# Hybrid attention step on one core: where a head's small products stand between the tile products

## The chip, the core and the metric

The kernel runs on one core of a Trainium2 chip. The core has a matrix engine (PE, whose weight loads the profile lists apart as PEld), a vector engine (DVE), a scalar engine (ACT), GpSimd (POOL) and SyncE (SP); each runs its own list of instructions in order, and they wait for each other through semaphores. The metric is the device time of one launch in microseconds (us), median of several runs. The profile is one execution taken with the hardware profiler.

## The reference

Two layers of a streaming encoder over 512 prompt rows and 8 x 16 sample rows (640 columns in all). What the change touches is the differential attention of eight heads per layer:

```python
s = einsum('bqhmd,bkhmd->bhmqk', q, k) * 64 ** -0.5      # two maps m per head
p = softmax(where(visible, s, NEG), axis=-1)
a = p[:, :, 0] - lam * p[:, :, 1]
o = einsum('bhqk,bkhe->bqhe', a, v)                       # per head, 128 wide
of = o * rsqrt(mean(o * o, axis=-1) + 1e-5) * g * (1 - lam_init)
```

Before the heads stands one projection `x @ w_in` (its part for the queries and keys of one head is 1024 x 256), behind them stand gates, a window attention, and a feed-forward part, which the change leaves alone.

## The kernel before, in words

Each large product is made of three products of rounded and remainder parts (`hi*hi`, `lo*hi`, `hi*lo`, lines L828 to L830). A feature tile is 128 output features by 640 columns in two halves of 320; one half is eight steps `k` of three products, written to banks 4 or 5 of PSUM. While head `h` is attended, PE computes the queries (`is_k` 0) and the keys (`is_k` 1) of head `h + 1`; in the last head of a layer two gate tiles (`early_gate`) take their place. So `tile(0, 0)`, `tile(0, 1)`, `tile(1, 0)` and `tile(1, 1)` are four half tiles in a row, and the attention of head `h` stands between and within them: a table such as `{(1, 4): f}` runs `f` ahead of step 4 of half 1. The order of PE's instructions is the order in which `head` writes them.

The small groups that matter here, with the line of their products:

- `output_transposes` (L1107): four transposes of the finished prompt output of head `h - 1` into bank 7. ACT's `output_copy` (L1735) takes the bank into `a_t` and counts `a_done`.
- `dec_transposes` (L1122): five transposes of the samples' probabilities `d_p`, for g = 0 and 1. The first four go to bank 6, the fifth to the first columns of bank 7. ACT's `dec_copy` (L1702) takes them.
- `dec_products` (L1132, L1140): the samples' values.
- `dec_map_sum` (L1150): the difference of the two maps of the samples, bank 0; DVE copies it to `d_out` (L2693), ACT squares it to `d_sq` (L1815).
- `unit_transpose` (L1191) and `unit_product` (L1202): the prompt's four units of 128 query rows, transposes to bank 6, ACT's `unit_copy` (L1686), values to bank 7. Units 0 and 1 go together, then 2, then 3.
- `mean_squares` (L1208): a product of `d_sq` with ones, bank 1; DVE takes it at L2616 and counts `dec_ms_copied`, and ACT goes on from there (L1715 and behind).

Each product on 32-bit values shows as two matrix instructions, each transpose as one. The waits ahead of a group are written in the group. The one that guards bank 7 stands inside `dec_transposes`:

```python
for t in range(5):
    if (g, t) == (0, 4):

        pe.wait_ge(a_done, n)
```

A tile of a gate waits for `gate_copied`, which ACT counts when it has copied the gate tile two places ahead (L1745); `early_gate(l, 2, 0)` in `last_head_end` thus waits until the tile just finished is copied.

Of the kernel before, what the change touches and what calls it, by code (L numbers as in the profile page):

```python
# [36 lines left out]
HEADS = 8  # L37
# [145 lines left out]
def build(nc, x_rows, x_cols, k_cache, v_cache, swa_kc, swa_vc, swa_k_keep, swa_v_keep, weights, cols,  # L183
# [4 lines left out]
    with ctx:  # L188
# [37 lines left out]
        for where, hi_at, lo_at in ((r_b, 0, 4096), (r_b, 20480, 24576), (r_b, 8192, 28672), (r_mix, 8192, 12288),  # L226
                                    (r_b, 32768, 36864), (r_mix, 12288, 16384), (r_mix, 4096, 8192)):
            n = len(w_hi)
# [298 lines left out]
        def nth(l, at_chunk, i=0):  # L527
            return l * (CHUNKS // 2) + (at_chunk // 2 + i)

        def gate_chunk(f):  # L530

            return f % 2, f // 2
# [5 lines left out]
        def b_chunk(f):  # L538
            return f % 2, 2 + f // 2
# [81 lines left out]
        def pairs_after(l, part):  # L621

            return pair_at(l, part, FF_PAIRS - 1)[0] + 1
# [49 lines left out]
        def wait_apart(eng, semaphore, value):  # L673


            eng.wait_ge(semaphore, value)
            eng.sem_inc(waits_passed, 1)
# [135 lines left out]
        def _(pe):  # L813
            mm = nc.tensor.matmul

            def feature_tile(s, n, hi, lo, which, part=None, between=None, slot=None, order=None):
                slot = s if slot is None else slot
                if order is None:
                    order = [(half, k) for half in ((0, 1) if part is None else (part,)) for k in range(KT)]
                if part != 1:  # L820
                    pe.wait_ge(w_ready[s], n + 1)
                for half, k in order:
                    out = PS[:, bank_of(which, half), 0:HALF]
                    c = slice(half * HALF, (half + 1) * HALF)
                    if between and (half, k) in between:
                        between[half, k]()
                    wh, wl = w_hi[slot][:, k * P:(k + 1) * P], w_lo[slot][:, k * P:(k + 1) * P]
                    mm(out, wh, hi[:, k, c], start=(k == 0), stop=False)  # L828
                    mm(out, wh, lo[:, k, c], start=False, stop=False)  # L829
                    last = mm(out, wl, hi[:, k, c], start=False, stop=(k == KT - 1))  # L830
                    if k == KT - 1:
                        last.then_inc((chunk_half_done if half == 0 else chunk_done)[s], 1)
# [229 lines left out]
            def rope_half_free(u, half):  # L1062

                pe.wait_ge(rope_swapped, 2 * u - 1 + half)
                pe.wait_ge(rope_cos_done, 2 * u - 1 + half)

            def head_tile(l, h, is_k, half, between):
                rope_half_free(l * ROPES + 2 * h + is_k, half)
                feature_tile(is_k, nth(l, AT_HEADS) + h, xt_hi, xt_lo, 0, half, between)

            def early_gate(l, f, half, between=None):

                s, i = gate_chunk(f)
                if f == 0:
                    rope_half_free(l * ROPES + 2 * HEADS, half)
                else:
                    pe.wait_ge(gate_copied, 7 * l + f)
                feature_tile(s, nth(l, AT_EARLY, i), xt_hi, xt_lo, 0, half, between)
# [31 lines left out]
            def dec_transposes(l, h, g):  # L1110
                n = l * HEADS + h
                pe.wait_ge(dec_exp, 2 * n + g + 1)
                if g == 0:

                    pe.wait_ge(unit_t_copied, 3 * n)
                else:
                    pe.wait_ge(dec_t_copied, 2 * n + 1)
# [4 lines that stand above are left out]
                    last = nc.tensor.transpose(flat[:, 6 * BANK + t * P:6 * BANK + (t + 1) * P],  # L1122
                                               d_p[:, g, t * P:(t + 1) * P], ident[:])
                last.then_inc(dec_t_ready, 1)
# [19 lines left out]
            def dec_map_sum(l, h):  # L1144

                n = l * HEADS + h
                pe.wait_ge(dec_o_copied, 2 * n + 2)
                pe.wait_ge(dec_sel_ready, n + 1)
                for g in range(2):
                    last = mm(PS[:, 0, g * 64:(g + 1) * 64], d_o[:, g, :], sel_r[:, g, :], start=True, stop=True)  # L1150
                last.then_inc(dec_ot_ready, 1)
# [29 lines left out]
            def unit_transpose(l, h, units):  # L1181
                n = l * HEADS + h
                pe.wait_ge(unit_probs, 4 * n + units[-1] + 1)
                if units[0] == 0:
                    pe.wait_ge(dec_t_copied, 2 * n + 2)
                else:
                    pe.wait_ge(unit_t_copied, 3 * n + units[0] - 1)
                at_col = 0
                for i in units:
                    for j in range(i + 1):  # L1190
                        last = nc.tensor.transpose(PS[:, 6, at_col:at_col + P],  # L1191
                                                   u_a_of[i][:, j * P:(j + 1) * P], ident[:])
                        at_col += P
                last.then_inc(unit_t_ready, 1)

            def unit_product(l, h, units):
                n = l * HEADS + h
                pe.wait_ge(unit_t_copied, 3 * n + max(units[-1], 1))
                for i in units:
                    for j in range(i + 1):  # L1200
                        t = (j if i == 0 else 1 + j) if i < 2 else j
                        last = mm(PS[:, 7, i * P:(i + 1) * P], u_at[max(i - 1, 0) % 2][:, t * P:(t + 1) * P],  # L1202
                                  rows[:, j, bass.ts(h, P)], start=(j == 0), stop=(j == i))
                last.then_inc(unit_pv, 1)

            def mean_squares(n):
                pe.wait_ge(dec_sq_ready, n + 1)
                mm(PS[:, 1, 0:P], ones[:], d_sq[:], start=True, stop=True).then_inc(dec_ms_ready, 1)  # L1208

            def head(l, h, p, first, more, uses):  # L1210

                n = l * HEADS + h

                def tile(is_k, half, between=None):
                    if more:
                        head_tile(l, h + 1, is_k, half, between)
                    else:
                        early_gate(l, is_k, half, between)

                tile(0, 0, None if first else {(0, 1): lambda: unit_transpose(l, h - 1, (3,)),  # L1220
                                               (0, 6): lambda: mean_squares(n - 1)})
                if not first:
                    unit_product(l, h - 1, (3,))
                else:
                    for r in range(RT):
                        wait_apart(pe, row_evacuated[r], l * GROUPS + 2)
                    pe.wait_ge(p5_copied, pairs_after(l, GATES))
                    pe.wait_ge(up_taken, 2 * pairs_after(l, GATES))
                    pe.wait_ge(c21_taken, pairs_after(l, GATES))
                    pe.wait_ge(consts_loaded, 16 * CONST_LOADS)  # L1230
                    pe.wait_ge(masks_ready, 2)
                dec_old_scores(l, h)
                dec_new_scores(l, h, p)
                tile(0, 1)
                unit_masks(l, h, (0, 1))
                unit_masks(l, h, (2,))
                unit_score(l, h, p, (0, 1))
                unit_score(l, h, p, (2,))
                if not first:
                    output_transposes(l, h - 1, 7)  # L1240
                tile(1, 0, {(0, 2): lambda: dec_transposes(l, h, 0), (0, 5): lambda: dec_transposes(l, h, 1)})
                dec_products(l, h)
                unit_score(l, h, p, (3,))
                unit_transpose(l, h, (0, 1))
                tile(1, 1, {(1, 4): lambda: dec_map_sum(l, h),
                            (1, 5): lambda: (unit_product(l, h, (0, 1)), unit_transpose(l, h, (2,)))})
                unit_product(l, h, (2,))

            def last_head_end(l):
                early_gate(l, 2, 0, {(0, 1): lambda: unit_transpose(l, HEADS - 1, (3,)),  # L1250
                                     (0, 6): lambda: mean_squares(l * HEADS + HEADS - 1)})
                unit_product(l, HEADS - 1, (3,))
                early_gate(l, 2, 1)

# [156 lines left out]
            for l in range(DEPTH):  # L1411
# [13 lines left out]
                pe.wait_ge(c11_taken, pairs_after(l, GATES))  # L1425

                all_heads(pe, l, head)
                last_head_end(l)

# [57 lines left out]
                for f in range(2 * PLAIN_B):  # L1487
                    n = nth(l, AT_BRANCH_B, b_chunk(f)[1])
# [2230 lines left out]
```

## Time and profile before

| | |
|---|---|
| runs | 2132.21, 2132.62, 2136.03 us; median 2132.62 |
| the profiled execution | 2132.67 us, of it 2130.9 us between the first and the last instruction |
| PE busy | 2116.2 us, 99% of the span |
| PEld busy | 1935.2 us, 91% |
| DVE, ACT busy | 1472.1 us (69%), 1230.6 us (58%) |
| heads of layer 1, of layer 2 | 129.5 to 349.4 us, 1191.6 to 1410.6 us |

A product's busy time reaches from its start to its modelled end, and products overlap: three in a row that start 0.147 us apart last 0.309 us each. So the time that a product costs is read from the distance between starts, and a stall from the start of the next weight load.

### The profile page before, as it was taken

How to read it: one execution, taken by the hardware profiler on the slowest of the kernel's cores; microseconds unless marked ns; L12 is line 12 of the kernel's file. 1: busy time of each engine (PE TensorE's matmuls, PEld its weight loads, DVE VectorE, ACT ScalarE, POOL GpSimd, SP SyncE). 2: the span in 40 equal slices, each digit the busy share in tenths (PEclk: the TensorE clock that was granted, in tenths of full speed). 3: DMA queues.
4: the chain of work that ended last, by engine and by line, in shares of the span. 5: the costliest groups of instructions: out<-in, count | busy, mean ns of one | idle time of the engine just before them, and what ended most of it. 6: DMA issues, size and time to landing. Idle time of an engine off the chain costs nothing.

```text
span 2130.9 us, 38215 instructions
## 1 busy us (share of the span) xinstructions
PE 2116.2 (99%) x15004; PEld 1935.2 (91%) x15004; DVE 1472.1 (69%) x2336; ACT 1230.6 (58%) x2493; POOL 64.6 (3%) x100
## 2 busy tenths in 40 slices
PE   9999999999999999999999999999999999999998
PEld 8998889999989898989889888899999898989897
DVE  6857777766879356665667577786778793566656
ACT  4457776696535356656234577766965353556561
POOL 1000000001000000000001000000110001000000
PEclk9999999999999999999999999999999999999999
DMA  7887562487861855454368765524778527544541
GB/s 251 237 291 257 204 219 107 146 250 218 222 228 50 237 158 171 146 168 139 109 188 240 279 251 211 211 79 156 244 206 246 204 73 224 166 165 154 168 149 70
DMA packets 100867, 399.27 MB, mean 187 GB/s; under 512 B 15273, under 2 KB 16937, under 8 KB 87601
## 3 DMA queue, kind: packets, MB, share of 16 engines
q1 hardware_dynamic: 67904, 191.55, 26.4%
q0 software_dynamic: 7936, 92.28, 17.1%
q10 hardware_dynamic: 24848, 112.99, 14.8%
q8 instruction: 120, 1.97, 0.4%
q14 instruction: 59, 0.48, 0.1%
HBM read 367.42 MB, written 118.23 MB: 228 GB/s over the span
## 4 chain that ended last, share of the span: by engine, by line
PE 96%; DMA 2%; ACT 1%; DVE 1%; issue 0%; ACTq 0%; DVEq 0%
PE PS L828 9%; PE PS L830 9%; PE PS L829 9%; PE PS L1049 6%; PE PS L1051 6%; PE PS L1050 6%; PE PS L917 5%; PE PS L919 5%; PE PS L918 5%; PE PS L863 4%; PE PS L862 4%; PE PS L861 4%; PE PS L987 3%; PE PS L988 3%; PE PS L989 3%; PE PS L1177 2%
## 5 line engine op out<-in xcount | busy, mean ns | idle before, releaser
L828 PE MATMUL PS<-xt_hi,w_hi 128*128 128x320 f32 x1184 | 382.3, 323 | 0.2
L830 PE MATMUL PS<-xt_hi,w_lo 128*128 128x320 f32 x1184 | 365.9, 309 | 0.0
L829 PE MATMUL PS<-xt_lo,w_hi 128*128 128x320 f32 x1184 | 365.7, 309 | 0.0
L2541 DVE TENSOR_TENSOR w_lo<-w_raw,w_hi 128x1024 fp32r<-128x1024 f32 x146 | 177.5, 1222 | 151.0 <-ACT w_hi L1579 149.4
L2548 DVE TENSOR_TENSOR w_lo<-w_raw,w_hi 128x1024 fp32r<-128x1024 f32 (+1 forms) x176 | 199.3, 1138 | 114.8 <-ACT w_hi L1595 114.5
L1579 ACT ACTIVATE w_hi<-w_raw 128x1024 fp32r<-128x1024 f32 x146 | 153.6, 1059 | 178.5 <-PE PS L1051 152.6
L828 PEld LDWEIGHTS PS<-xt_hi,w_hi 128*128 128x128 f32 x1184 | 222.8, 188 | 5.4 <-issue 4.3
L829 PEld LDWEIGHTS PS<-xt_lo,w_hi 128*128 128x128 f32 x1184 | 223.0, 188 | 0.1
L830 PEld LDWEIGHTS PS<-xt_hi,w_lo 128*128 128x128 f32 x1184 | 222.3, 188 | 0.0
L1595 ACT ACTIVATE w_hi<-w_raw 128x1024 fp32r<-128x1024 f32 (+1 forms) x176 | 172.2, 984 | 86.1 <-PE PS L989 66.3
L1049 PE MATMUL PS<-w_hi,act_a_hi 128*128 128x512 f32 x480 | 187.9, 391 | 2.3 <-DVE rows L3007 2.3
L1051 PE MATMUL PS<-w_hi,act_a_lo 128*128 128x512 f32 x480 | 187.0, 390 | 0.0
L1050 PE MATMUL PS<-w_lo,act_a_hi 128*128 128x512 f32 x480 | 186.9, 389 | 0.0
L1628 ACT ACTIVATE rope_s<-PS 32x320 f32<-32x320 f32 x352 | 150.7, 428 | 56.4 <-DVE z_all L2532 28.4
L919 PE MATMUL PS<-t_hi,w_lo 128*128 128x320 f32 x448 | 138.5, 309 | 0.0
L917 PE MATMUL PS<-t_hi,w_hi 128*128 128x320 f32 x448 | 138.5, 309 | 0.0
L918 PE MATMUL PS<-t_lo,w_hi 128*128 128x320 f32 x448 | 138.5, 309 | 0.0
L1049 PEld LDWEIGHTS PS<-w_hi,act_a_hi 128*128 128x128 f32 x480 | 90.1, 188 | 21.4 <-issue 3.3
L1051 PEld LDWEIGHTS PS<-w_hi,act_a_lo 128*128 128x128 f32 x480 | 90.1, 188 | 18.8
L1050 PEld LDWEIGHTS PS<-w_lo,act_a_hi 128*128 128x128 f32 x480 | 90.2, 188 | 18.1
L919 PE MATMUL PS<-xt_hi,w_lo 128*128 128x320 f32 x336 | 103.9, 309 | 0.0
L918 PE MATMUL PS<-xt_lo,w_hi 128*128 128x320 f32 x336 | 103.9, 309 | 0.0
(391 smaller groups left out, 5095.0 us busy)
## 6 DMA issues: line engine op xcount, KB each, us to landing
w_raw<-in_weights SPq DMA_DIRECT2D x186, 512.0 KB, 4.8
kc<-in_k_cache ACTq DMA_DIRECT2D x32, 1024.0 KB, 7.7
vc<-in_v_cache ACTq DMA_DIRECT2D x16, 2048.0 KB, 8.7
w_raw<-up_sums SPq DMA_DIRECT2D x112, 256.0 KB, 2.9
up_sums<-in_up_blocks POOLq DMA_DIRECT2D x24, 1024.0 KB, 9.0
w_raw<-in_up_blocks SPq DMA_DIRECT2D x84, 256.0 KB, 2.8
down_sums<-in_down_blocks POOLq DMA_DIRECT2D x16, 1024.0 KB, 11.3
w_raw<-in_down_blocks SPq DMA_DIRECT2D x32, 512.0 KB, 3.4
```

Source lines behind the costliest of these rows:

```text
L828: mm(out, wh, hi[:, k, c], start=(k == 0), stop=False)
L829: mm(out, wh, lo[:, k, c], start=False, stop=False)
L830: last = mm(out, wl, hi[:, k, c], start=False, stop=(k == KT - 1))
L917: mm(up_bank(x), wh, moving[0][:, k], start=first and k == 0, stop=False, skip_group_check=True)
L918: mm(up_bank(x), wh, moving[1][:, k], start=False, stop=False, skip_group_check=True)
L919: last = mm(up_bank(x), wl, moving[0][:, k], start=False, stop=(k == KH - 1), skip_group_check=True)
L1049: mm(out, xh, wh, start=(k == 0), stop=False)
L1050: mm(out, xh, wl, start=False, stop=False)
L1051: last = mm(out, xl, wh, start=False, stop=(k == KT - 1))
L1595: fn(w_hi[RING[slot]][:, c], raw[:, j, c], ACT.Copy).then_inc(ring_hi, 1)
L2541: v.tensor_tensor(w_lo[slot][:], raw[:, raw_of(s, n)[0], :], w_hi[slot][:].bitcast(F32), ALU.subtract)\
L2548: v.tensor_tensor(w_lo[slot][:, c], raw[:, raw_of_ring(g)[0], c], w_hi[slot][:, c].bitcast(F32), ALU.subtract).then_inc(ring_ready, 1)
```

## The change

In `head` and `last_head_end` four groups move; no product, wait or transfer is added or removed.

1. `unit_product` of unit 2 moves from the end of a head (behind `tile(1, 1)`) to behind the first step of the next tile, ahead of `unit_transpose` of unit 3.
2. `mean_squares` moves from ahead of step 6 of `tile(0, 0)` to its end, ahead of `unit_product` of unit 3.
3. `dec_transposes` for g = 0 moves from ahead of step 2 of `tile(1, 0)` to ahead of the tile, that is, to right behind `output_transposes`; for g = 1 from ahead of step 5 to ahead of step 4.
4. `dec_map_sum` moves from ahead of step 4 of `tile(1, 1)` to ahead of step 5, between `unit_product` of units 0 and 1 and `unit_transpose` of unit 2.

```diff
-                tile(0, 0, None if first else {(0, 1): lambda: unit_transpose(l, h - 1, (3,)),
-                                               (0, 6): lambda: mean_squares(n - 1)})
+                tile(0, 0, None if first else {(0, 1): lambda: (unit_product(l, h - 1, (2,)),
+                                                                unit_transpose(l, h - 1, (3,)))})
                 if not first:
+                    mean_squares(n - 1)
                     unit_product(l, h - 1, (3,))
...
                 if not first:
                     output_transposes(l, h - 1, 7)
-                tile(1, 0, {(0, 2): lambda: dec_transposes(l, h, 0), (0, 5): lambda: dec_transposes(l, h, 1)})
+                dec_transposes(l, h, 0)
+                tile(1, 0, {(0, 4): lambda: dec_transposes(l, h, 1)})
                 dec_products(l, h)
                 unit_score(l, h, p, (3,))
                 unit_transpose(l, h, (0, 1))
-                tile(1, 1, {(1, 4): lambda: dec_map_sum(l, h),
-                            (1, 5): lambda: (unit_product(l, h, (0, 1)), unit_transpose(l, h, (2,)))})
-                unit_product(l, h, (2,))
+                tile(1, 1, {(1, 5): lambda: (unit_product(l, h, (0, 1)), dec_map_sum(l, h),
+                                             unit_transpose(l, h, (2,)))})
 
             def last_head_end(l):
-                early_gate(l, 2, 0, {(0, 1): lambda: unit_transpose(l, HEADS - 1, (3,)),
-                                     (0, 6): lambda: mean_squares(l * HEADS + HEADS - 1)})
+                early_gate(l, 2, 0, {(0, 1): lambda: (unit_product(l, HEADS - 1, (2,)),
+                                                      unit_transpose(l, HEADS - 1, (3,)))})
+                mean_squares(l * HEADS + HEADS - 1)
                 unit_product(l, HEADS - 1, (3,))
```

PE's list of instructions in the middle of a head, from the output's transposes on, before the change (an instruction with its waits stands apart from the rest of its group; `w_hi_56` and `w_lo_58` are the weights of the keys' tile):

```order
L1107 MATMUL PS<-ident,o_n 128x128 [waits o_n_ready]
L1107 MATMUL PS<-ident,o_n 128x128 x3
L828 MATMUL PS<-xt_hi,w_hi_56 128x320 [waits w_ready1,rope_cos_done,rope_swapped]
L829 MATMUL PS<-xt_lo,w_hi_56 128x320
L830 MATMUL PS<-xt_hi,w_lo_58 128x320
L828 MATMUL PS<-xt_hi,w_hi_56 128x320
L829 MATMUL PS<-xt_lo,w_hi_56 128x320
L830 MATMUL PS<-xt_hi,w_lo_58 128x320
L1122 MATMUL PS<-ident,d_p 128x128 [waits unit_t_copied,dec_exp]
L1122 MATMUL PS<-ident,d_p 128x128 x3
L1122 MATMUL PS<-ident,d_p 128x128 [waits a_done]
```

The same place with the change:

```order
L1107 MATMUL PS<-ident,o_n 128x128 [waits o_n_ready]
L1107 MATMUL PS<-ident,o_n 128x128 x3
L1122 MATMUL PS<-ident,d_p 128x128 [waits unit_t_copied,dec_exp]
L1122 MATMUL PS<-ident,d_p 128x128 x3
L1122 MATMUL PS<-ident,d_p 128x128 [waits a_done]
L828 MATMUL PS<-xt_hi,w_hi_56 128x320 [waits w_ready1,rope_cos_done,rope_swapped]
L829 MATMUL PS<-xt_lo,w_hi_56 128x320
L830 MATMUL PS<-xt_hi,w_lo_58 128x320
```

The six tile products that stood between the output's transposes and the samples' transposes now stand behind both.

PE's list at the end of a layer's last head before the change, from the last product of `tile(1, 1)` on (`u_at_167` holds unit 2, `u_a_164` unit 3, and the weights `w_hi_55` and `w_lo_57` are those of gate tile 2):

```order
L830 MATMUL PS<-xt_hi,w_lo_58 128x320
L1202 MATMUL PS<-rows,u_at_167 128x128 [waits unit_t_copied]
L1202 MATMUL PS<-rows,u_at_167 128x128 x2
L828 MATMUL PS<-xt_hi,w_hi_55 128x320 [waits w_ready0,gate_copied]
L829 MATMUL PS<-xt_lo,w_hi_55 128x320
L830 MATMUL PS<-xt_hi,w_lo_57 128x320
L1191 MATMUL PS<-ident,u_a_164 128x128 [waits unit_t_copied,unit_probs]
L1191 MATMUL PS<-ident,u_a_164 128x128 x3
```

The same place with the change:

```order
L830 MATMUL PS<-xt_hi,w_lo_58 128x320
L828 MATMUL PS<-xt_hi,w_hi_55 128x320 [waits w_ready0,gate_copied]
L829 MATMUL PS<-xt_lo,w_hi_55 128x320
L830 MATMUL PS<-xt_hi,w_lo_57 128x320
L1202 MATMUL PS<-rows,u_at_167 128x128 [waits unit_t_copied]
L1202 MATMUL PS<-rows,u_at_167 128x128 x2
L1191 MATMUL PS<-ident,u_a_164 128x128 [waits unit_t_copied,unit_probs]
L1191 MATMUL PS<-ident,u_a_164 128x128 x3
```

The values of unit 2 have moved from ahead of the product that waits for `gate_copied` to behind it. In the other heads they move in the same way past a tile product that waits for the weights and the rotation instead.

## Rows read from the trace of the kernel before

**Rows 1.** The page: span, and busy time, share and instructions of PE.

```profile
span 2130.9 us, 38215 instructions
PE 2116.2 (99%) x15004; PEld 1935.2 (91%) x15004; DVE 1472.1 (69%) x2336; ACT 1230.6 (58%) x2493; POOL 64.6 (3%) x100
```

**Rows 2.** Layer 1's heads: PE, PEld, DVE, ACT, POOL busy; clock, DMA share, GB/s.

```profile
129.50:349.40 219.90, 219.78 (x2169) 191.35 (x2169) 163.41 (x391) 158.26 (x404) 0.00 (x0) 1.00 0.60 218
```

**Rows 3.** PE in order of time: start, us, engine, line; groups of nine and six.

```profile
203.41 0.31 PE L830 MATMUL PS<-xt_hi,w_lo 128*128 128x320 f32 x1
203.56 0.83 PE L1202 MATMUL PS<-rows,u_at 128*128 128x128 f32 x6
...
204.70 0.31 PE L829 MATMUL PS<-xt_lo,w_hi 128*128 128x320 f32 x1
...
205.72 0.31 PE L830 MATMUL PS<-xt_hi,w_lo 128*128 128x320 f32 x1
205.87 0.83 PE L1202 MATMUL PS<-rows,u_at 128*128 128x128 f32 x6
...
206.69 0.30 PE L829 MATMUL PS<-xt_lo,w_hi 128*128 128x320 f32 x1
```

**Rows 4.** The same view around the mean squares' product.

```profile
207.71 0.31 PE L830 MATMUL PS<-xt_hi,w_lo 128*128 128x320 f32 x1
...
209.47 0.31 PE L830 MATMUL PS<-xt_hi,w_lo 128*128 128x320 f32 x1
209.62 0.38 PE L1208 MATMUL PS<-d_sq,ones 128*128 128x128 f32 x2
209.76 0.39 PE L828 MATMUL PS<-xt_hi,w_hi 128*128 128x320 f32 x1
209.99 0.30 PE L829 MATMUL PS<-xt_lo,w_hi 128*128 128x320 f32 x1
```

**Rows 5.** Weight loads in order of time, around the transposes of the fourth head.

```profile
219.87 0.19 PEld L828 LDWEIGHTS PS<-xt_hi,w_hi 128*128 128x128 f32 x1
...
220.71 0.62 PEld L1122 LDWEIGHTS PS<-ident,d_p 128*128 128x128 f32 x5
221.30 0.19 PEld L828 LDWEIGHTS PS<-xt_hi,w_hi 128*128 128x128 f32 x1
```

**Rows 6.** ACT in order of time, the same head.

```profile
217.39 0.20 ACT L1694 ACTIVATION_READ_ACCUMULATOR d_p<-PS,small 128x1 f32 x1
...
220.26 0.69 ACT L1735 ACTIVATE a_t<-PS,g_sub 128x512 f32<-128x512 f32 x1 [0.46 <-PE PS L1107]
...
221.60 0.71 ACT L1702 ACTIVATE d_pt<-PS 128x640 f32<-128x640 f32 x1
```

**Rows 7.** All of L1107: who waited for it, us in total, times.

```profile
  ACT a_t L1735: 7.9, 14
```

**Rows 8.** Weight loads at the end of layer 1's last head.

```profile
343.13 0.78 PEld L1202 LDWEIGHTS PS<-rows,u_at 128*128 128x128 f32 x6
344.22 0.19 PEld L828 LDWEIGHTS PS<-xt_hi,w_hi 128*128 128x128 f32 x1 [0.32 <-ACT rope_s L1745]
...
344.63 0.50 PEld L1191 LDWEIGHTS PS<-ident,u_a 128*128 128x128 f32 x4
```

**Rows 9.** ACT there (the gate's copy), and all tile products L828 that waited for it.

```profile
343.47 0.70 ACT L1745 ACTIVATE rope_s<-PS 128x640 f32<-128x640 f32 x1 [0.47 <-PE PS L830]
...
  ACT rope_s L1745: 0.6, 2
```

**Rows 10.** DVE there: the probabilities of unit 3.

```profile
342.24 0.75 DVE L2610 SCALAR_TENSOR_TENSOR u_a<-u_p,small 128x512 f32<-128x512 f32 x1
```

**Rows 11.** DVE in the third head: the low weights, the mean squares' reading.

```profile
203.39 1.22 DVE L2541 TENSOR_TENSOR w_lo<-w_raw,w_hi 128x1024 fp32r<-128x1024 f32 x1 [0.24 <-ACT w_hi L1579]
...
210.83 0.28 DVE L2616 TENSOR_SCALAR d_ms<-PS 128x128 f32<-128x128 f32 x1
```

**Rows 12.** PE in the fourth head: the masks that wait for the samples' exponentials.

```profile
217.84 0.26 PE L1167 MATMUL PS<-mask_cols 128*128 128x64 bf16 x3
```

## The prediction

> **What bounds the kernel now.** I read the page first: PE is busy for 2116.2 of 2130.9 us, 99% [rows 1]. A busy PE need not be at its peak, so the next view was busy time over the heads, where the whole change lies: 219.78 of 219.90 us with a product under way at granted clock 1.00 (the higher level, 2.4 GHz), while DVE is busy for 163 and ACT for 158 us [rows 2]. PE's list sets the time there; only two things can move it: what a product costs next to its neighbours, and a wait that PE reaches too early. For both I read PE and its weight loads in order of time.
>
> **What standing next to each other is worth.** Tile products start 0.147 us apart: twelve steps from 207.71 to 209.47 [rows 4]. The cost of a small group is the time from the tile product ahead of it to the second tile product behind it, less the two steps that lie there anyway. The mean squares' two instructions: 209.99 - 209.47 - 0.294 = 0.226 us [rows 4]. The values of unit 2, six: 206.69 - 205.72 - 0.294 = 0.676. Units 0 and 1 with the transposes of unit 2, nine in one group: 204.70 - 203.41 - 0.294 = 0.996 [rows 3]. That is 0.113, 0.113 and 0.111 for each instruction, however long the group. The tile product behind a group does look 0.08 longer (0.39 against 0.31), but the last small one ahead of it takes correspondingly less: it starts 0.14 after the first of two small ones that need 0.11 each [rows 4]. From two to nine instructions the line is 0.110 each and 0.006 for the group. The change joins 4 groups to others in each of 16 heads, 64 in all: 64 x 0.006 = 0.4 us less. With times to 0.01 us this is between 0 and twice that.
>
> **The samples' transposes for g = 0.** The fifth waits for `a_done`, which ACT counts when it has copied the output's transposes of the same head out of bank 7. Before, six tile products gave ACT time for this. In the fourth head the load behind the four output transposes starts at 219.87 [rows 5]; ACT starts its copy at 220.26 and ends at 220.95 [rows 6], and the samples' five loads start at 220.71, the fifth some 0.15 + 3 x 0.11 = 0.48 later, at 221.19 [rows 5]: 0.24 to spare. (The steps: five loads from 220.71 to the next one at 221.30 make one of 0.15 and four of 0.11.) With the change the first of the five loads stands at 219.87 and the fifth at 219.87 + 4 x 0.11 = 220.31, while ACT's copy still hangs on the output's transposes and ends at 220.95. How fast a load follows an end of ACT shows where PE waits for ACT already: the gate's copy ends at 343.47 + 0.70 = 344.17, the load starts at 344.22 [rows 8, 9], 0.05 later. So the fifth load starts at 221.00 and PE stands for 221.00 - 220.31 = 0.69 us. Nothing fills it: the whole next tile is queued behind. It happens in each head with an output to transpose ahead of its samples, 14 of 16 (ACT waited for L1107 in 14 cases [rows 7]; the first head of a layer has none, the last output stands elsewhere): 14 x 0.69 = 9.7 us.
>
> On the load there is a rule to weigh. At the gate's wait the load L828 itself is held to 344.22, although its weights were not what was waited for [rows 8]. The Trainium skill's page "TensorE: Matmul & The Clock Gate", section "Architectural detail: the array is 16× 32×32, not 1× 128×128", says that PE's queue is a partial reorder window, which can pull weight loads ahead of matmuls in flight. By that rule the fifth load could go ahead of the wait, and only its product be held; the sum would be 1.5 us less (rivals). The row differs from it, and I take the row: the wait holds the load as well.
>
> **The values of unit 2.** They moved behind a tile product that may have to wait. In 14 heads that product needs low weights which DVE finishes at 203.39 + 1.22 = 204.61 in the third head [rows 11]; with the change it stands right behind the L830 at 205.72 [rows 3], and its load a step ahead, 1.1 us after the weights. No cost. In the last head of each layer the product waits for the gate's copy. Before, the six loads of the values start at 343.13; at 0.15 + 5 x 0.11 the next load was due at 343.83 and came at 344.22 [rows 8]: PE stood for 0.39, and the values covered the rest. The copy starts when the tile ahead is done (ACT waits 0.47 for L830 [rows 9]), so the change doesn't move it. PE now stands from 343.13 + 0.15 on and does the values afterwards: the cover is gone, and each such head pays the 0.676 of the values. Both layers show this wait [rows 9]: 2 x 0.67 = 1.3 us.
>
> **The rest.** The samples' probabilities for g = 0 end at 217.59, 2.3 us ahead of their new place [rows 5, 6]. For g = 1 the wait is for ACT's copy of g = 0, done at 221.60 + 0.71 = 222.31 [rows 6]; the group's load is due at 221.00 + 0.11 + 12 x 0.147 = 222.87, so the stall has bought the slack (0.56). The maps' difference only comes later than its inputs did; its new place in the last head is some nine tile steps and seven small ones ahead of 343.13 [rows 8], 343.13 - 1.32 - 0.77 = 341.0, while DVE turns to its result only when unit 3 is combined, at 342.24 + 0.75 = 342.99 [rows 10]. The mean squares come six tile steps, 0.88 us, later. They ended at 209.62 + 0.38 = 210.00 and DVE read them at 210.83 [rows 4, 11]; the new end is 210.88, so the reading slips by up to 0.1, and with it the samples' exponentials of the next head. These end at 217.59 against masks at 217.84 [rows 6, 12]: 0.25 in hand, no cost.
>
> **Sum.** Against the profiled execution's 2132.67 (span 2130.9), which stands 0.05 above the median of the runs: 2132.67 + 9.7 + 1.3 - 0.4 = 2143.3 us, 0.5% slower.
>
> **Rivals.**
> - The fifth load goes ahead of the wait and only its product is held: each stall is one step of 0.11 shorter, 0.58 us, 14 x 0.58 = 8.1, sum 2132.67 + 8.1 + 1.3 - 0.4 = 2141.7 us. Against it stands the held load at the gate [rows 8]. (This is what the Trainium skill's rule above would do.)
> - No stall at the fifth transpose, because PE goes on with the tile behind it: 2132.67 + 1.3 - 0.4 = 2133.6, no change. Against it: at the gate PE held the transposes of unit 3 too, whose input DVE had finished at 342.99 [rows 10] and which started at 344.63, after the tile products ahead of them [rows 8]. PE doesn't pass a wait.
> - The mean squares are late for the masks: each 0.1 us beyond the 0.25 in hand costs 14 x 0.1, sum 2144.7 at 0.1. The rows leave 0.15 of the 0.25.
> - Faster: a boundary between small and tile products costs more than the 0.006. Read from the longer product alone it is 0.08, and 64 x 0.08 = 5.1 us gives 2138.6, still slower. It decides from (11.0 + 4.3) / 64 = 0.24 us a boundary, more than the whole 0.226 of the mean squares' group; then 2128.4 or less. Nothing speaks for it.
>
> **How the numbers follow.** The forecast has 0.82, a load ahead 0.07, late masks 0.05, no stall 0.04, a costly boundary 0.02. Low end: stalls of 0.58 and 0.8 for the boundaries, 2132.67 + 8.1 + 1.3 - 0.8 = 2141.3; high end: 14 x 0.80 (one more step of 0.11 behind the wait) + 1.3, and 0.1 of late masks, 2132.67 + 11.2 + 1.3 + 1.4 = 2146.6. I widen the low end by the 0.4 by which two of the runs differ, to 2140.9. Faster and slower are meant beyond 0.2% (4.3 us), about what a measurement can tell from no change. Only the no-stall case is the same, and 0.01 more for noise: 0.02 faster, 0.05 same, 0.93 slower.
>
> **What would show it.** The loads L1122 of g = 0 should stand right behind L1107, four of five in a row, then a gap of about 0.69 us that ACT's L1735 ends, in 14 heads; the waits should list L1122 for L1735 with some 9 to 10 us, where before there was no such entry. L828 should wait about 1.1 us for L1745 twice, followed by the values. Groups joined together should cost 0.11 per instruction. The prediction is wrong if the fifth transpose follows without a gap, if products behind it run in the meantime, or if a later wait of the head (dec_t_copied, the masks) opens as well.

## The result, and the profile after

| | before | after |
|---|---|---|
| runs | 2126.82 to 2136.36 us (6) | 2138.33 to 2142.63 us (6) |
| median | 2132.41 us | 2139.84 us |
| ratio | | 1.0033, 95% interval 1.0018 to 1.0048 |
| profiled execution | 2132.67 us, span 2130.9 us | 2139.42 us, span 2137.6 us |
| granted clock, mean over the span | 0.999 | 0.999 |

Slower by 0.33% (the ratio is taken from all the runs; that of the two medians is 1.0035), as forecast in sign, but 2139.84 lies 1.1 us below the low end of the range (2140.9) and 3.5 below the predicted time. What stands behind these 3.5 us is the question of the experiments.

The page of the changed kernel, span and engines, against [rows 1]:

```profile
span 2137.6 us, 38215 instructions
PE 2117.0 (99%) x15004; PEld 1932.6 (90%) x15004; DVE 1473.5 (69%) x2336; ACT 1230.2 (58%) x2493; POOL 65.1 (3%) x100
```

PE's busy time grew by 0.8 us and the span by 6.7: the time went into waits. PE's waits in the changed kernel (line waited at, what ended it: us in total, times, longest us):

```profile
PE PS L1122 <- ACT a_t L1737: 6.0, 14, 0.4
PE PS L1090 <- DMA kc<-in_k_cache: 1.6, 2, 1.2
PE PS L828 <- ACT rope_s L1747: 1.6, 2, 0.8
...
PE PS L1049 <- DVE rows L3009: 0.9, 1, 0.9
```

In ACT's and DVE's part of the kernel the line numbers are two higher than before: L1737 is the copy of bank 7 (before: L1735), L1747 the gate's copy. The first and the third line are the two stalls of the forecast, 14 and 2 in number. The view gives 0.4 us for one, since it counts from the modelled end of the products ahead. The weight loads, for which the forecast was made, show more of its length:

```profile
PEld PS L1122 <- ACT a_t L1737: 9.3, 14, 0.7
...
PEld PS L828 <- ACT rope_s L1747: 2.1, 2, 1.1
```

Weight loads in order of time in the fourth head, to be held against [rows 5]:

```profile
220.38 0.42 PEld L1107 LDWEIGHTS PS<-ident,o_n 128*128 128x128 f32 x4 [0.60 <-issue]
220.77 0.47 PEld L1122 LDWEIGHTS PS<-ident,d_p 128*128 128x128 f32 x4
221.90 0.14 PEld L1122 LDWEIGHTS PS<-ident,d_p 128*128 128x128 f32 x1 [0.66 <-ACT a_t L1737]
221.97 0.19 PEld L828 LDWEIGHTS PS<-xt_hi,w_hi 128*128 128x128 f32 x1
```

ACT in the same head, against [rows 6]:

```profile
221.16 0.69 ACT L1737 ACTIVATE a_t<-PS,g_sub 128x512 f32<-128x512 f32 x1 [0.35 <-PE PS L1107]
...
222.43 0.71 ACT L1704 ACTIVATE d_pt<-PS 128x640 f32<-128x640 f32 x1
```

The samples' loads follow the output's at 220.77, four of five run, and the fifth stands until ACT's copy has ended: 221.16 + 0.69 = 221.85, load at 221.90, again 0.05 later. It should have come at about 220.77 + 3 x 0.11 + 0.11 = 221.21, so it is 0.69 late. The load itself is held, not only its product, and no tile product passes it. At the end of layer 1's last head, against [rows 8]:

```profile
347.00 0.19 PEld L830 LDWEIGHTS PS<-xt_hi,w_lo 128*128 128x128 f32 x1
348.24 0.19 PEld L828 LDWEIGHTS PS<-xt_hi,w_hi 128*128 128x128 f32 x1 [1.05 <-ACT rope_s L1747]
348.64 0.78 PEld L1202 LDWEIGHTS PS<-rows,u_at 128*128 128x128 f32 x6
```

The gap ahead of the gate's tile grew from 0.32 to 1.05 us, and the values that used to fill it come behind it. (Gate tile 2 waits until ACT has counted two copies in the layer. The second is that of gate tile 1, the tile just ahead and not one two places ahead.)

How long all of this makes the heads is read from PE's first masks (L1167) and the last output transposes (L1107) of a layer. Layer 1 before:

```profile
135.68 0.35 PE L1167 MATMUL PS<-mask_cols 128*128 128x64 bf16 x6
...
354.23 0.60 PE L1107 MATMUL PS<-ident,o_n 128*128 128x128 f32 x4
```

and after:

```profile
135.31 0.35 PE L1167 MATMUL PS<-mask_cols 128*128 128x64 bf16 x6
...
358.91 0.60 PE L1107 MATMUL PS<-ident,o_n 128*128 128x128 f32 x4
```

From start to start that is 218.55 and 223.60 us: 5.05 more, and 5.03 in layer 2, 10.1 in all. But the span grew by 6.7 only. Outside the heads, where both programs are the same, the profiled execution after was some 3.3 us shorter. Theory A: that part differs from execution to execution whatever the kernel, and the forecast was added to an execution in which it was long. Theory B: time is given back there, since during the stalls transfers and the other engines get ahead.

### The profile page after: what moved, and what is told of

Read it like the earlier page. It is cut to its first block, busy times and chain, and to the rows that moved or that the text cites. A ratio compares the mean times of both kernels' runs of the same rounds, so it can differ in the third digit from the quotient of the medians.

```text
span 2137.6 us, 38215 instructions
## 1 busy us (share of the span) xinstructions
PE 2117.0 (99%) x15004; PEld 1932.6 (90%) x15004; DVE 1473.5 (69%) x2336; ACT 1230.2 (58%) x2493; POOL 65.1 (3%) x100
## 4 chain that ended last, share of the span: by engine, by line
PE 96%; DMA 2%; ACT 2%; DVE 0%; issue 0%; DVEq 0%; ACTq 0%
PE PS L828 9%; PE PS L829 9%; PE PS L830 9%; PE PS L1049 7%; PE PS L1051 7%; PE PS L1050 7%; PE PS L919 5%; PE PS L917 5%; PE PS L918 5%; PE PS L863 4%; PE PS L861 4%; PE PS L862 4%; PE PS L989 3%; PE PS L987 3%; PE PS L988 3%; PE PS L1177 2%
## 5 line engine op out<-in xcount | busy, mean ns | idle before, releaser
L828 PE MATMUL PS<-xt_hi,w_hi 128*128 128x320 f32 x1184 | 377.3, 319 | 1.6 <-ACT rope_s L1747 1.6
L828 PEld LDWEIGHTS PS<-xt_hi,w_hi 128*128 128x128 f32 x1184 | 222.8, 188 | 5.6 <-issue 3.1
L1049 PE MATMUL PS<-w_hi,act_a_hi 128*128 128x512 f32 x480 | 188.0, 392 | 0.9 <-DVE rows L3009 0.9
L1049 PEld LDWEIGHTS PS<-w_hi,act_a_hi 128*128 128x128 f32 x480 | 90.2, 188 | 19.8 <-issue 1.8
L1050 PEld LDWEIGHTS PS<-w_lo,act_a_hi 128*128 128x128 f32 x480 | 90.2, 188 | 18.1
```

Of the source, the lines that this page charges most:

```text
L1049: mm(out, xh, wh, start=(k == 0), stop=False)
L1050: mm(out, xh, wl, start=False, stop=False)
```

## The experiments

Diffs of dt_only, up_only, maps_ms and best are against the kernel before, the others against the changed kernel where nothing else is said. All heads below run from a layer's first L1167 to the last single transpose L1107 (0.33 us behind the row's start); "rest" is the span less the heads of both layers. Profiled executions:

| kernel | heads, layer 1 / 2 | span | rest | ratio to before (95%) |
|---|---|---|---|---|
| before | 218.87 / 218.89 | 2130.9 | 1693.1 | |
| null | 218.88 / 218.88 | 2128.4 | 1690.6 | 0.9996 (0.9986 to 1.0006) |
| null_2 | 218.91 / 218.90 | 2127.7 | 1689.9 | one run |
| after | 223.93 / 223.92 | 2137.6 | 1689.8 | 1.0033 (1.0018 to 1.0048) |
| again | 223.96 / 223.94 | 2138.4 | 1690.5 | 1.0043 (1.0027 to 1.0060) |
| dt_only | 223.47 / 223.46 | 2137.9 | 1691.0 | 1.0041 (1.0027 to 1.0055) |
| dt_back | 219.39 / 219.40 | 2130.1 | 1691.3 | 1.0001 (0.9991 to 1.0011) |
| fifth_stays | 220.90 / 220.89 | 2135.8 | 1694.0 | 1.0021 (1.0011 to 1.0032) |
| fifth5 | 219.34 / 219.35 | 2126.3 | 1687.6 | one run |
| copy_twice | 227.23 / 227.24 | 2144.6 | 1690.1 | 1.0070 (1.0056 to 1.0085) |
| up_only | 219.56 / 219.55 | 2131.5 | 1692.4 | 0.9995 (0.9986 to 1.0004) |
| maps_ms | 218.76 / 218.77 | 2126.1 | 1688.6 | one run |
| best | 218.23 / 218.22 | 2126.3 | 1689.9 | 0.9989 (0.9979 to 0.9999) |

The two layers of one execution agree within 0.02 us, and the three traces of the kernel before within 0.04. The heads thus show differences of 0.1 us a layer that the time of a launch can't.

**null and null_2: the kernel before, unchanged, profiled anew.**

> The kernel before, unchanged, once more. In the two traces at hand PE's time from the first masks of a layer's heads to the last output transposes grew by 5.05 and 5.03 us, 10.1 in all, but the span only by 6.7: the waits for the first inputs, for the key cache ahead of the heads (L1090) and for the rows in the second half of a layer (L1049) came out 3.3 us shorter. Theory A (scatter): these waits differ from run to run whatever the kernel; here some of them differ from the first trace by 1 us or more, up or down, and the heads take 218.87 and 218.89 us again to 0.05. Theory B (given back): longer heads leave the transfers more time, so the later waits shrink with the change; here, with heads as before, the waits are those of the first trace (1.8 us at L1049 in layer 1, 1.8 at L1090 in layer 2) to 0.3 us. Time 2132 to 2133 us by both.

> The kernel before, profiled once more. Heads of 218.88 us in both layers; the rest of the span anywhere between 1689.8 and 1694.0 us, as waits for transfers ahead of a layer's heads and in its second half fall. If the rest was shorter in the changed kernel because time was given back behind the heads, this run's should be at 1690.6 to 1693.1, as the two traces of before, and not below.

The heads were the same to 0.04 us, but the time expected for null, 2132 to 2133 us, was missed. The rest was 1693.1, 1690.6 and 1689.9 us in three executions of one program, the last within 0.1 of the changed kernel's. Where it differs shows in PE's waits. Before:

```profile
PE PS L1049 <- DVE rows L3007: 2.3, 2, 1.8
PE PS L1090 <- DMA kc<-in_k_cache: 1.8, 1, 1.8
```

null:

```profile
PE PS L1049 <- DVE rows L3007: 1.6, 2, 1.3
```

null_2:

```profile
PE PS L1090 <- DMA kc<-in_k_cache: 1.5, 1, 1.5
```

L1090 is a head's product with the cached keys, and waits for their transfer; these waits stand in a layer's first head, ahead of the masks from which the heads are counted. L1049 stands in the second half of a layer and waits until DVE has taken rows. They come and go: 1.8 and 2.3 us, none and 1.6, 1.5 and none. In the changed kernel one wait of 1.2 us at L1090 falls in layer 1, at 130.0 us, ahead of everything that was changed; before it was not there.

These waits are nearly all of the 3.3 us. From the last output transpose of layer 1 to the first masks of layer 2 there were 842.33 us before, 838.91 in null, 840.36 in null_2, 839.02 after and 840.44 in again. The waits at L1049 and L1090 in that stretch were 3.57, 0.32, 1.53, 0.35 and 1.64 us; without them 838.6 to 838.8 us are left in all five, with long heads as with short ones. The profiled execution before thus had 3.2 us of waits there that the one after had not.

Null's median of 12 runs was 2129.30, beside 2129.19 of 30 runs of the kernel before on that chip; the profiled execution of before, 2132.67, was among its longer ones.

The longer executions also show a lower mean granted clock. Of the 55 runs of the kernel before in the three later comparisons, 43 at 0.999 took 2127.3 to 2134.1 us, eight at 0.998 took 2131.2 to 2134.6, and four at 0.997 took 2135.9 to 2137.6. One trace, that of fifth_stays (below), shows what can stand behind this. In the second half of layer 1 PE waited 3.38 us for DVE's rows:

```profile
625.17 0.47 PE L1049 MATMUL PS<-w_hi,act_a_hi 128*128 128x512 f32 x1 [3.38 <-DVE rows L3011]
...
628.32 0.63 PE L1050 MATMUL PS<-w_lo,act_a_hi 128*128 128x512 f32 x1
628.75 0.63 PE L1051 MATMUL PS<-w_hi,act_a_lo 128*128 128x512 f32 x1
```

From 626.6 to 630.0 us the granted clock was 0.51, about the lower of its two levels (1.2 GHz), and the products started 0.43 us apart instead of 0.23. In the twelve other traces the clock fell only behind PE's last product. Whether the other long executions had such a stretch is not shown.

**dt_only: move 3 alone, the samples' transposes.**

```diff
                 if not first:
                     output_transposes(l, h - 1, 7)
-                tile(1, 0, {(0, 2): lambda: dec_transposes(l, h, 0), (0, 5): lambda: dec_transposes(l, h, 1)})
+                dec_transposes(l, h, 0)
+                tile(1, 0, {(0, 4): lambda: dec_transposes(l, h, 1)})
```

> Before, with the samples' transposes alone moved (g = 0 to right behind the output's transposes, g = 1 one step ahead). If the fifth transpose's wait for a_done is the cause: 14 gaps of 0.69 us ahead of it, heads longer by 7 x 0.65 = 4.5 to 4.9 us in each layer, 9 to 9.7 in all, and the span longer by that under theory A (give or take 3 us of scatter), by about two thirds of it under theory B. If the values of unit 2 or the mean squares are the larger part: under 2 us.

The heads grew by 4.60 and 4.57 us. With 7 stalls in a layer that is 0.655 each. The stalled load is 0.69 late, but the load behind it follows after 0.07 instead of 0.11 us (the rows of the fourth head above: 221.90, 221.97). PE's waits listed the same stall as after:

```profile
PE PS L1122 <- ACT a_t L1736: 6.0, 14, 0.4
```

**dt_back: the changed kernel with move 3 undone.**

```diff
-                dec_transposes(l, h, 0)
-                tile(1, 0, {(0, 4): lambda: dec_transposes(l, h, 1)})
+                tile(1, 0, {(0, 2): lambda: dec_transposes(l, h, 0), (0, 5): lambda: dec_transposes(l, h, 1)})
```

> The changed kernel with the samples' transposes put back, the other three moves kept. If a_done's wait is the cause: no such gap, heads longer only by the 0.67 us of the values of unit 2 in each layer's last head, less some 0.05 in each of 8 heads for the maps' difference (as the trace after has it), so 0.2 to 0.4 us a layer, and a time within 1 us of before. If the stall comes from the other moves: 4 us a layer stay.

No wait at L1122 was left, the heads stood 0.52 above before, and the time of a launch could not be told from before's. So move 3 carries most of the loss: 4.5 of 5.05 us a layer. The 0.52 was more than the 0.2 to 0.4 that I expected; the single moves below explain it.

**fifth_stays: four transposes moved, the fifth left where it was.**

```diff
-                dec_transposes(l, h, 0)
-                tile(1, 0, {(0, 4): lambda: dec_transposes(l, h, 1)})
+                dec_transposes(l, h, 0, range(4))
+                tile(1, 0, {(0, 2): lambda: dec_transposes(l, h, 0, range(4, 5)),
+                            (0, 4): lambda: dec_transposes(l, h, 1)})
```

The last argument picks the transposes; not shown is the edit in `dec_transposes` that takes it and lets the fifth alone signal ACT.

> The changed kernel, but of the samples' five transposes for g = 0 only four stand behind the output's transposes, the fifth, which waits for a_done, at its old place two tile steps later. If the wait alone is the cause: heads within 0.1 us a layer of those without the move of the transposes. If the nine transposes standing together, or the tile that follows them, is what costs: some 4 us a layer stay.

The expectation was missed: the wait for ACT's copy of bank 7 was gone, but the heads stood 2.0 us a layer above before, 1.5 above dt_back. The loads show the reason. The group of g = 1 now came only two steps behind the fifth transpose, and waits for ACT's copy of g = 0, which needs that transpose:

```profile
220.67 0.19 PEld L830 LDWEIGHTS PS<-xt_hi,w_lo 128*128 128x128 f32 x1
221.09 0.53 PEld L1122 LDWEIGHTS PS<-ident,d_p 128*128 128x128 f32 x5 [0.24 <-issue]
```

0.42 us from the tile's load to the group's, and 0.42 to 0.44 in all 16 heads. The view names no releaser here ("issue"), but in all 16 the load starts 0.11 us behind the end of that copy. It was my experiment's own new wait, and left open whether the wait or the joining cost the time.

**fifth5: fifth_stays with g = 1 at its old place too (diff against fifth_stays).**

```diff
-                            (0, 4): lambda: dec_transposes(l, h, 1)})
+                            (0, 5): lambda: dec_transposes(l, h, 1)})
```

> Changed kernel with the samples' fifth transpose of g = 0 at its old place ahead of step 2 of tile(1, 0), and g = 1 at its old place ahead of step 5; only the first four transposes of g = 0 stand right behind the output's. If the wait for a_done, reached too early, is all that makes move 3 slow: no wait at the fifth and none at g = 1 (where fifth_stays had one), heads as with move 3 undone, 219.4 +- 0.2 us a layer. If joining the transposes of g = 0 to the output's costs by itself, or a wait that the fifth_stays trace showed at g = 1 was not the cause of its 1.5 us a layer: 220 us or more.

In the same head of fifth5:

```profile
220.88 0.19 PEld L830 LDWEIGHTS PS<-xt_hi,w_lo 128*128 128x128 f32 x1
221.03 0.61 PEld L1122 LDWEIGHTS PS<-ident,d_p 128*128 128x128 f32 x5
```

0.15 us and no idle time; the heads stood at 219.34, 0.05 below dt_back. Four of the five transposes next to the output's cost nothing and bring next to nothing; the waits alone make move 3 slow.

**copy_twice: the changed kernel, with one more ACT copy of bank 7 (into a scratch tile) ahead of the one that counts a_done.** The added work is not part of the computation.

```diff
                 wait_apart(act, o_t_ready, l * HEADS + h + 1)
+                fn(o_sq[:].rearrange("p t n -> p (t n)"), PS[:, bank, :], ACT.Copy)
                 fn(a_t[:, h, 0:SEQ], PS[:, bank, :], ACT.Copy, scale=g_sub[:, bass.ds(l, 1)])\
                     .then_inc(a_done, 1)
```

> The changed kernel, with one more copy of bank 7 by ACT (into o_sq, which is rewritten before it is read) ahead of the one that counts a_done. ACT's copy of 128x512 occupies it for some 0.6 us, so a_done comes 0.5 to 0.6 us later. If the stall follows the end of that copy: each of the 14 gaps grows by as much, the heads by 3.5 to 4.2 us a layer over the changed kernel, the time by 7 to 8.4 us. If the fifth transpose waits for something else (the tile's own waits, the order of loads): no growth.

ACT in the fourth head:

```profile
221.09 0.60 ACT L1737 ACTIVATE o_sq<-PS 128x512 f32<-128x512 f32 x1 [0.36 <-PE PS L1107]
221.58 0.68 ACT L1738 ACTIVATE a_t<-PS,g_sub 128x512 f32<-128x512 f32 x1
```

and the fifth load:

```profile
222.31 0.14 PEld L1122 LDWEIGHTS PS<-ident,d_p 128*128 128x128 f32 x1 [1.15 <-ACT a_t L1738]
```

The copy starts 221.58 - 221.09 = 0.49 us behind the added one, the gap grows by 1.15 - 0.66 = 0.49, and the heads by 3.3 us a layer, 7 x 0.47, a little under the expected 3.5 to 4.2. The stall follows a_done one to one. The rest was 1690.1 us, no shorter than after's although the stalls were longer by 70%: against theory B.

**up_only: move 1 alone, the values of unit 2.**

```diff
-                tile(0, 0, None if first else {(0, 1): lambda: unit_transpose(l, h - 1, (3,)),
+                tile(0, 0, None if first else {(0, 1): lambda: (unit_product(l, h - 1, (2,)),
+                                                                unit_transpose(l, h - 1, (3,))),
...
-                unit_product(l, h, (2,))
...
-                early_gate(l, 2, 0, {(0, 1): lambda: unit_transpose(l, HEADS - 1, (3,)),
+                early_gate(l, 2, 0, {(0, 1): lambda: (unit_product(l, HEADS - 1, (2,)),
+                                                      unit_transpose(l, HEADS - 1, (3,))),
```

> Before, with the values of unit 2 alone moved behind the first step of the next tile. By the prediction 0.67 us in the last head of each layer, where the gate's copy is waited for, and nothing elsewhere: heads 219.5 to 219.6 us a layer. If joining the six values and four transposes saved a boundary's 0.08 us: 0.6 us a layer less than that, so 218.9.

The heads grew by 0.69 and 0.66 us, all of it in the last head: 0.67 each, as worked out. In the other seven the move changed nothing.

**maps_ms: moves 2 and 4 alone**, the mean squares at the tile's end and the maps' difference between the units' groups (the two edits of the change, without the others).

> Moves 2 and 4 alone. From the single runs: the maps' difference beside units 0 and 1 gives 8 x 0.05 = 0.4 us a layer less, the late mean squares make the masks of one head a layer wait 0.1 us longer, so heads of about 218.6 us a layer (218.88 before), and no longer wait at the gate's tile. If the 0.1 us a layer that the run with move 3 undone left unexplained belongs to the mean squares: 218.7. If it belongs to the pair of move 1 with the others: 218.55.

The heads fell by 0.11 us a layer, less than expected. In each of the 16 heads the 24 products of `tile(1, 1)`, with what stands between them, took 4.851 us from first to last start against 4.887 before: joining the maps' difference to the other two groups is worth 0.036 a head, 0.29 a layer. (I had expected 0.05, from rows around the group alone.) The mean squares gave part of it back. In the third head of layer 1 and the seventh of layer 2 the masks' loads came apart. Before and in maps_ms, the third head:

```profile
190.33 0.18 PEld L1167 LDWEIGHTS PS<-mask_cols 128*128 128x128 bf16 x3
190.55 0.49 PEld L1177 LDWEIGHTS PS<-k_t,q_t 64*64 64x64 f32 x18
```

```profile
189.51 0.28 PEld L1167 LDWEIGHTS PS<-mask_cols 128*128 128x128 bf16 x3
189.84 0.27 PEld L1177 LDWEIGHTS PS<-k_t,q_t 64*64 64x64 f32 x10
```

0.22 us from the masks to the scores became 0.33, since the masks wait for the samples' exponentials, which come behind the mean squares; in best, which has move 4 without move 2, it was 0.23. 0.29 less 0.1 would be a fall of 0.19, and 0.11 was measured; the other 0.08, some 0.01 a head, shows in no single wait. With these sizes move 3 undone should give 0.67 - 0.29 + 0.1 = 0.48 a layer, or 0.67 - 0.11 = 0.56 with the fall as measured here; 0.52 was measured.

**best: move 4 alone, and in the last head the transposes of unit 3 ahead of the gate's tile, to cover its wait.** Move 4's edit, as in the change, is left out here:

```diff
             def last_head_end(l):
-                early_gate(l, 2, 0, {(0, 1): lambda: unit_transpose(l, HEADS - 1, (3,)),
-                                     (0, 6): lambda: mean_squares(l * HEADS + HEADS - 1)})
+                unit_transpose(l, HEADS - 1, (3,))
+                early_gate(l, 2, 0, {(0, 6): lambda: mean_squares(l * HEADS + HEADS - 1)})
```

> Before, with two things: the maps' difference between the values of units 0 and 1 and the transposes of unit 2 (move 4 alone), which in the trace after costs 1.39 us with its neighbours where the two groups cost 1.44 before; and in a layer's last head the transposes of unit 3 ahead of the product that waits for the gate's copy, to fill its 0.40 us. Both together: heads 0.7 to 0.8 us a layer shorter than before (218.1), 1.5 us in all, which the runs can't tell from no change. If a boundary is worth nothing at all: 0.4 us a layer.

Its weight loads at the end of layer 1's last head, against [rows 8]:

```profile
342.55 0.78 PEld L1202 LDWEIGHTS PS<-rows,u_at 128*128 128x128 f32 x6
343.25 0.47 PEld L1191 LDWEIGHTS PS<-ident,u_a 128*128 128x128 f32 x4
343.69 0.19 PEld L828 LDWEIGHTS PS<-xt_hi,w_hi 128*128 128x128 f32 x1
```

The gap ahead of the gate's tile is filled: 0.40 us a layer, and 0.29 from move 4, less some hundredths, make 0.65 a layer, a little under the 0.7 to 0.8 expected. The ratio, 0.9989 with an interval that ends at 0.9999, agrees with 1.3 of 2130 us, which is 0.06%; that it beats the kernel before in the time of a launch is at the edge of what the runs show.

**again: the changed kernel once more.**

> The changed kernel once more. Theory A: heads (first masks to last output transposes of a layer) 223.9 us in both layers again, against 218.9 of before, so 10.1 us more; the waits for first inputs, for the key cache and for the rows come out in other places and sizes than in the first trace after, and the median against before is 10 us slower, give or take 3. Theory B: the same short waits as in the first trace after, 7 us slower.

The heads came out alike to 0.03 us. Its median of 7 runs was 2139.43 against 2130.43 of 24 runs of before: 9.0 us, where the first comparison gave 2139.84 - 2132.41 = 7.4. The growth of the heads, 10.1 us or 0.47%, lies within both intervals, near the upper end of the first.

## Why the prediction was wrong, and where it was right

**The base of the sum and its scatter failed.** The step that failed is "Against the profiled execution's 2132.67", together with the range, which allowed for the scatter of that base by "the 0.4 by which two of the runs differ". That two of the three runs shown agreed so closely was chance; the third, 2136.03, stood 3.4 us above them, and the range left it out. Runs of the kernel before went from 2126.82 to 2137.56 us, and its medians in four comparisons were 2132.41, 2129.19, 2130.43 and 2127.35 (the last a single run). Unchanged heads with a rest of 1693.1, 1690.6 and 1689.9 show that this scatter lies outside the heads, in the traces mostly in two waits.

The growth itself was nearly right: 10.6 us forecast, 10.1 in the heads. On the medians of the two larger comparisons, 2130.43 of 24 runs and 2129.19 of 30, the recorded sum gives 2141.0 and 2139.8; with the measured 10.1 it gives 2140.5 and 2139.3, against medians of the changed kernel of 2139.84 and 2139.43. The 7.4 us of the first comparison are less than the heads' growth because its median of before stood 2 to 3 us above the two larger ones, while the changed kernel's two medians differ by 0.4. The experiments ran on three chips, and that of the first comparison is not on record; how much of the difference between the medians of before is the chip's was not tried.

The trace of before could have warned me: 1.8 us at L1090 for a transfer and 2.3 at L1049 stand in its waits, and nothing says that they come each time. With half of these 4.1 us as possibly absent, the low end would have been 2140.9 - 2.05 = 2138.9 and the range would have held the result; but that half is chosen with the result known.

**Theory B is not needed.** Kernels with long heads (after, again, dt_only, copy_twice) had a rest of 1689.8 to 1691.0, those within 0.7 us a layer of before 1687.6 to 1693.1. The ranges overlap; the shortest rest belongs to fifth5, which has no stall at L1122, and the longest, 1694.0, to fifth_stays, which has waits in all 16 heads and the stretch at the lower clock. In launches, theory B had some two thirds of the growth left over (the expectation of dt_only); for copy_twice that would be 11.1 of 16.7 us, and its interval, 0.56 to 0.85% of 2130 us, reaches from 11.9 to 18.1. The intervals of again and dt_only are too wide to tell. That a part is given back can't be excluded. Why the transfer of the cached keys and DVE's rows come earlier in one execution than in another was not tried.

**The stall, 14 x 0.69 = 9.7:** right in place, number, cause and lateness of the load. Net it is 0.655, 9.2 in all: the load behind follows 0.04 closer. The rival "load goes ahead of the wait" (8.1) has the load at work while ACT still copies; the fifth load starts 0.05 us behind ACT's end, in 14 cases, so the wait holds the load too. The Trainium skill, "TensorE: Matmul & The Clock Gate", section "Architectural detail: the array is 16× 32×32, not 1× 128×128", says that PE's queue can pull weight loads ahead of matmuls in flight. That sentence names no semaphore wait, and in none of the 14 cases here was the load pulled ahead of one. No product behind the stall ran in the meantime either, so the rival without a stall is excluded too.

**The values, 2 x 0.67 = 1.3:** right; 0.69 and 0.66 by up_only.

**The joining, 64 x 0.006 = 0.4:** the sum was about right and its even spread was not. The maps' difference gave 0.036 in each of 16 heads, 0.6 in all; the other joints gave less than 0.01 each by the same reading. (The groups joined are 62, not 64: in a layer's first head no output transposes stand ahead of the samples'.) The costly boundary is excluded with them.

**The mean squares:** "0.25 in hand, no cost" held in 14 heads and failed in two, where the masks' wait grew by 0.1, one of the signs of being wrong that the prediction had named. I had read the slack in the fourth head and taken it for all. Two times 0.1 is a seventh of the rival's 1.4.

**g = 1:** right; in the fourth head after, the load starts 0.55 us behind the end of ACT's copy, where 0.56 was forecast. In fifth_stays, with the fifth transpose two tile steps later, this wait did open.

The terms as measured alone, 9.2 + 1.35 - 0.2, make 10.3; the changed kernel's heads grew by 10.1. dt_only and dt_back, which hold the four moves between them, add up to 10.2, so half of this 0.2 lies in how moves 1, 2 and 4 act together. The other half I did not find.

## What to carry to other kernels

Here small products cost about their own time wherever they stood, so ask of such a move to "next to others" which waits it reaches earlier, and what used to cover them: a product pulled ahead by six tile steps (0.88 us) ran into a copy that could not end earlier. A wait inside a group moves with the group; splitting the group, as fifth5 does, keeps it off the path. And a forecast of 0.5% needs a base from several executions: lay out which waits of the trace come and go, and let the range hold all the runs at hand and the size of these waits.

## What the runs showed of the hardware

A semaphore wait reads longer by the weight loads than by the products: the same 14 stalls read 6.0 us in PE's waits and 9.3 in PEld's, and the heads grew by 9.2 in dt_only; here the loads' gap is close to the price. Behind a stall one transpose's load is followed by a tile's load after 0.07 instead of 0.11 us, which agrees with the 0.04 by which each stall costs less than the 0.69. Stalls of up to 1.15 us in copy_twice left the granted clock at 1.00 through the heads, the higher of the two levels (2.4 GHz); a wait of 3.38 us in fifth_stays was followed by 3.4 us at about the lower one (1.2 GHz).
